# First modulation and projections by quarters of the features, and one round of modulation steps on GpSimd

## What is computed

```python
c_act = silu(c)
for l in range(2):
    mod = c_act @ w_ada[l] + b_ada[l]                # 6 * 1024 columns
    sh1, sc1, gt1, sh2, sc2, gt2 = split(mod, 6)
    h = rmsnorm(x, g_norm1[l]) * (1 + sc1) + sh1
    x = x + gt1 * hybrid_mixer(h, w_in[l], ...)      # four kinds of attention, A to D
    h = rmsnorm(x, g_norm2[l]) * (1 + sc2) + sh2
    x = x + gt2 * grouped_moe(h, ...)
return rmsnorm(x, g_final)
```

## Time and profile before

| | us |
|---|---|
| median of 3 runs | 997.39 (996.74 to 999.74) |
| the profiled execution | 999.34 |
| its span | 997.5 |
| mean granted TensorE clock | 0.983 |
| TensorE busy | 944.5 |
| VectorE busy | 562.0 |
| ScalarE busy | 298.8 |
| GpSimd busy | 61.7 |

### The profile page before, as it was taken

How to read it: one execution, slowest core, us unless ns; L and a number is a source line. 1 busy time by engine, 2 the same in 40 slices (tenths; PEclk the granted TensorE clock), 3 DMA queues, 4 the chain that set the end, 5 groups by cost and what they waited for, 6 DMA issues and landing times.

```text
span 997.5 us, 13699 instructions
## 1 busy us (share of the span) xinstructions
PE 944.5 (95%) x5131; PEld 558.7 (56%) x5131; DVE 562.0 (56%) x1319; ACT 298.8 (30%) x773; POOL 61.7 (6%) x69
## 2 busy tenths in 40 slices
PE   4799999999999899999999999998999979999996
PEld 1344464567644548666754445565774446667572
DVE  1469897779545633223285789785762355223227
ACT  3131224467322221112142122336762122112113
POOL 0001001100000010000300010110000001001012
PEclk9999999999999799999999999999999988999998
DMA  9988417721373789999686471143006058999936
GB/s 352 361 297 280 173 64 253 253 65 46 124 297 95 297 332 404 417 420 367 204 330 239 151 271 64 64 169 24 2 2 274 28 235 310 392 420 420 415 139 235
DMA packets 88529, 231.59 MB, mean 232 GB/s; under 512 B 37768, under 2 KB 52472, under 8 KB 73984
## 3 DMA queue, kind: packets, MB, share of 16 engines
q1 hardware_dynamic: 79536, 198.21, 53.6%
q0 software_dynamic: 5760, 20.97, 5.8%
q10 hardware_dynamic: 3168, 11.54, 2.8%
HBM read 212.85 MB, written 22.57 MB: 236 GB/s over the span
## 4 chain that ended last, share of the span: by engine, by line
PE 87%; DVE 5%; DMA 3%; issue 2%; SPq 1%; POOL 1%; ACT 1%; DVEq 0%; ACTq 0%; POOLq 0%
PE bank L1305 80%; PE bank L1322 5%; PE bank L1642 2%; DMA wbuf<-in_w_ada 2%; DMA shared<-y_rows,ints 1%; DVE shared L826 1%; SPq L1833 1%; DVE x L1258 1%; DVE shared L950 0%; POOL shared L531 0%; DVE x L1267 0%; DVE tok L950 0%; DVE tok L1031 0%; DMA y_rows<-tok 0%; PE bank L1683 0%
## 5 line engine op out<-in xcount | busy, mean ns | idle before, releaser
L1305 PE MATMUL bank<-shared,wbuf 128*128 128x512 f32 (+2 forms) x640 | 239.0, 531 | 0.0
L1305 PE MATMUL bank<-wbuf,shared 128*128 128x512 f32 (+3 forms) x672 | 199.2, 494 | 0.0
L1305 PE MATMUL bank<-shared 128*128 128x128 f32 (+9 forms) x1348 | 183.5, 340 | 1.4 <-ACT tok L567 0.9
L1305 PEld LDWEIGHTS bank<-shared,wbuf 128*128 128x128 f32 (+1 forms) x640 | 109.8, 189 | 123.8 <-issue 115.6
L1305 PEld LDWEIGHTS bank<-shared 128*128 128x128 f32 (+3 forms) x1348 | 138.4, 186 | 46.2 <-issue 40.9
L1305 PEld LDWEIGHTS bank<-wbuf,shared 128*128 128x128 f32 (+1 forms) x672 | 99.5, 178 | 78.6 <-issue 75.0
L1197 DVE TENSOR_TENSOR tring<-bank,tring 128x256 f32<-128x256 f32 x22 | 9.3, 425 | 144.7 <-ACT tring L737 144.7
L567 ACT ACTIVATE shared<-bank 128x512 f32<-128x512 f32 (+3 forms) x60 | 33.7, 561 | 139.7 <-PE bank L1305 138.8
L826 DVE SCALAR_TENSOR_TENSOR shared<-wbuf,small,shared 128x2048 f32<-128x2048 f32 x29 | 69.3, 2388 | 10.4 <-DMA wbuf<-in_w_ada 9.0
L737 ACT ACTIVATE tring<-bank 128x256 f32<-128x256 f32 x22 | 8.5, 384 | 196.7 <-PE bank L1305 196.7
L1305 PE MATMUL bank<-shared,tring 128*128 128x512 f32 x136 | 61.8, 597 | 3.1 <-DVE tring L1243 1.9
(11 more groups left out here) (267 smaller groups left out, 1091.4 us busy)
## 6 DMA issues: line engine op xcount, KB each, us to landing
wbuf<-in_w_ada SPq DMA_DIRECT2D x36, 1024.0 KB, 6.9
shared<-in_w_gate SPq DMA_DIRECT2D x20, 1024.0 KB, 14.8
shared<-in_w_up SPq DMA_DIRECT2D x20, 1024.0 KB, 17.6
shared<-in_w_down SPq DMA_DIRECT2D x20, 1024.0 KB, 16.6
shared<-in_w_ada SPq DMA_DIRECT2D x12, 1024.0 KB, 9.8
wbuf<-in_w_in SPq DMA_DIRECT2D x8, 1536.0 KB, 6.8
wbuf<-in_w_gate SPq DMA_DIRECT2D x12, 1024.0 KB, 7.0
wbuf<-in_w_up SPq DMA_DIRECT2D x12, 1024.0 KB, 10.5
```

What stands on the lines that cost most here:

```text
L1305: return nc.tensor.matmul(dst, lhsT, rhs, start=first, stop=last)
```

## The change

- **The start, layer 0.** x is loaded in two halves. The first 2048 columns of w_ada come by quarters: quarter g is the 256 sh1 columns and the 256 sc1 columns of features 2g and 2g+1 for all 1024 rows, two tiles of 1 MiB, in pieces of 1 KB. Behind each quarter comes a piece of w_in: the rows of features 2g and 2g+1, 672 columns (qD, kvD, qi, ki). The narrow columns come last. hT is first filled with the turned x alone. Quarter 0 goes through TensorE as before; quarters 1 to 3 are eight products each on VectorE (`first_products`), summed over partitions on TensorE (`first_turn`). Then VectorE and ScalarE scale and shift one feature block each in place.
- **The first projections, layer 0.** qi0, qi1, qD0, qD1 and kvD are accumulated in five banks at once, two feature blocks after each quarter (`stream`). kiwi follows, then vDT, cq0, wiT, four scores of block 1, cq1, four scores, ckv. Layer 1 keeps its order.
- **Round 1, both layers.** Steps 8 to 15 leave VectorE. GpSimd does each as a multiply in place and an add (`late_step`), three ahead of the squares of the latents and five behind, before the rotary key. Tiles have five places, two of them in the room of qC, kC and of qA, kA; ScalarE waits for GpSimd's third step before it writes qA. The sum of round 1 on TensorE moves behind vC.
- **SP.** The order of loads follows: in layer 0 chunk 2 of w_in gets room of its own and goes early; tiles 8 and 9 go ahead of tile 3, in layer 1 behind a wait for the end of the combination.
- Some semaphores of VectorE's and ScalarE's own steps are replaced by `link`, which does the same.

The core of the diff:

```diff
+FIRST_COLS = [(OFF["dq"], 672)] + INDEX_PARTS[1:]
+FIRST_BLOCKS = [(("qi", 0), 384), (("qi", 1), 512), (("qD", 0), 0), (("qD", 1), 128), ("kvD", 256)]
+FIRST_KIWI, FIRST_WIDTH = 640, 744
+QUARTERS = 4
...
-ADA_SLOTS = 3
-SLOT_OF = [b % 3 for b in range(14)] + [0, 1] + [b % 2 for b in range(KT)]
+ADA_SLOTS = 5
+SLOT_OF = [b % 3 for b in range(KT)] + [4, 3, 4, 0, 1, 0, 1, 0] + [b % 2 for b in range(KT)]
...
+def steps_to(b):
+
+    return 2 * (b - KT) + 1 if on_pool(b) else b + 1 if b < KT else b - KT + 1
...
+    jobs += [(("qi", m), "act") for m in range(2)]
+    if l == 0:
+        jobs += [(("qD", 0), "act"), (("qD", 1), "act"), ("kvD", "act"), ("kiwi", "act"), ("vDT", "act")]
+        jobs += [(("cq", 0), "act"), ("wiT", "dve")]
+        jobs += idx_jobs(1, ("cq", 1), "ckv")
+    else:
+        jobs += [("kiwi", "act"), (("qD", 0), "act"), ("wiT", "dve")]
+        jobs += idx_jobs(1, ("qD", 1), "kvD")
+        jobs += [(("cq", 0), "act"), ("vDT", "act"), (("cq", 1), "act"), ("ckv", "act")]
...
+        if now[0] == 0 and n == 2:
+            return part(29, 6).rearrange("p h n -> p (h n)").rearrange("p (k n) -> p k n", k=KT)
...
+                def late_step(b):
+
+                    need(pool, ada_landed[SLOT_OF[b]], 16 * (SLOT_OF[0:b].count(SLOT_OF[b]) + 1))
+                    w, k, total = ada_slot(b), b % KT, ada_sum[1]
+                    if k == 0:
+                        nc.gpsimd.tensor_scalar(total, w, cact[:, 0:1], None, ALU.mult).then_inc(late_ada, 1)
+                    else:
+                        nc.gpsimd.tensor_scalar(w, w, cact[:, k:k + 1], None, ALU.mult).then_inc(late_ada, 1)
+                        need(pool, late_ada, 2 * k)
+                        nc.gpsimd.tensor_tensor(total, total, w, ALU.add).then_inc(late_ada, 1)
+
+                if l == 0:
+                    pool.wait_ge(c_ready, 1)
+                for b in range(KT, KT + 3):
+                    late_step(b)
                 for m, name in enumerate([("cq", 0), ("cq", 1), "ckv"]):
                     wait_drained(pool, name)
                     src = cqT[:, m, :] if m < 2 else ckvT
                     nc.gpsimd.tensor_tensor(sqT[:, m, :], src, src, ALU.mult).then_inc(cq_squared, 1)
 
+                for b in range(KT + 3, 2 * KT):
+                    late_step(b)
                 need(pool, cq_squared, 3)
-                need(pool, sum_used, 2)
+                need(pool, sum_used, 1)
                 wait_drained(pool, "kiwi")
                 need(pool, rope_landed, 32)
                 nc.gpsimd.tensor_tensor(krT[0:32, :], krT[0:32, :], cosT[0:32, :], ALU.mult).then_inc(krope_ready, 1)
...
+                    need(act, late_ada, steps_to(KT + 2))
                     drain_pair(("qA", m), qA, m)
...
+
+                for k in range(KT):
+                    wait_first_tile(dve, 2 * g + k // 4)
+                    w = first_tile(2 * g + k // 4)[:, k % 4 * 512:(k % 4 + 1) * 512]
+                    if k == 0:
+                        link(nc.vector.tensor_scalar(first_row, w, cact[:, 0:1], None, ALU.mult))
+                    else:
+                        last = nc.vector.scalar_tensor_tensor(out=first_row, in0=w, scalar=cact[:, k:k + 1], in1=first_row,
+                                                              op0=ALU.mult, op1=ALU.add)
+                        if k < KT - 1:
+                            link(last)
+                last.then_inc(first_row_ready, 1)
...
+                if l == 0:
+                    for k in range(0, KT, 2):
+                        wait_filled(dve, ("h1", k))
+                        nc.vector.tensor_copy(hT[:, k, :], bank(("h1", k))[:, :]).then_inc(dve_drained, 1)
+                    dve.wait_ge(first_turned, 1)
+                    link(nc.vector.tensor_copy(biasT[:, 0:16], banks[7][:, 0:16]))
+                    dve.wait_ge(first_used, 1)
+                    nc.vector.tensor_copy(first_row, banks[6][:, :]).then_inc(first_row_ready, 1)
+                    dve.wait_ge(norm1_landed, 16)
+                    for g in range(QUARTERS):
+                        if g > 0:
+                            first_products(g)
+                        first_scale(g)
+                        k = 2 * g
+                        wait_drained(dve, ("h1", k))
+                        nc.vector.tensor_scalar(hT[:, k, :], hT[:, k, :], scaleT[:, k:k + 1], modT[:, k:k + 1],
+                                                ALU.mult, ALU.add).then_inc(first_h, 1)
...
                 index_sums(1, 0)
                 index_sums(1, 4)
                 dve.wait_ge(consts_landed, CONSTS * 16)
                 top(1)
-                for b in range(KT, 12):
-                    ada_step(b)
                 index_sums(2, 0)
-                for b in range(12, 14):
-                    ada_step(b)
                 index_sums(2, 4)
                 top(2)
                 mod_row(0)
                 index_sums(3, 0)
-                for b in range(14, 2 * KT):
-                    ada_step(b)
...
+
+            def first_turn(g):
+
+                pe.wait_ge(first_row_ready, g + 1)
+                for j in range(4):
+                    at = 64 * (g + 1) + NE * j
+                    last = mm(banks[7][:, at:at + NE], first_row[:, j * P:(j + 1) * P], collect[:, :] if g == 0 else ones[:, 0:NE])
+                last.then_inc(first_rows_turned, 1)
+
+            def stream(k, blocks):
+
+                for name, at in blocks:
+                    last = mm(bank(name)[:, :], first_win[:, k, at:at + P], hT[:, k, :], k == 0, k == KT - 1)
+                    if k == KT - 1:
+                        last.then_inc(psum_filled, 1)
...
+            first_turn(0)
+            for name, _ in FIRST_BLOCKS:
+                wait_bank(pe, name)
+            for g in range(QUARTERS):
+                pe.wait_ge(win_landed[g] if g < 2 else first_win_landed[g - 2], 16)
+                pe.wait_ge(first_h, 2 * g + 2)
+                stream(2 * g, FIRST_BLOCKS)
+                stream(2 * g + 1, FIRST_BLOCKS[0:2])
+                if g < QUARTERS - 1:
+                    first_turn(g + 1)
+                stream(2 * g + 1, FIRST_BLOCKS[2:])
...
+                if l == 0:
+                    need(pe, narrow_landed, (len(INDEX_PARTS) - 1) * 16)
+                    features("kiwi", 104, lambda k: first_win[:, k, FIRST_KIWI:FIRST_KIWI + 104], hT, KT)
+                    turn_vDT()
+                    need(pe, win_landed[2], 16)
+                    project(("cq", 0), 2, 0, P)
+                    turn_wiT()
+                    host(("cq", 1), 2, P, 1, 0)
+                    host("ckv", 2, 256, 1, 4)
...
-                sum_mods(1)
                 wait_drained(pe, ("vA", TT - 1))
...
+                sum_mods(1)
                 need(pe, latents_ready, 1)
...
+            def load_first_ada(n):
+                g, b = divmod(n, 2)
+                columns = w_ada[0:1].rearrange("a (k p) (c n) -> p (a k) c n", p=P, n=D)
+                for c in range(2):
+                    sp.dma_start(first_tile(n).rearrange("p (k c n) -> p k c n", k=4, c=2)[:, :, c, :],
+                                 columns[:, 4 * b:4 * b + 4, c, 2 * g * P:(2 * g + 2) * P]).then_inc(first_ada_landed[max(n - 1, 0)], 16)
+
+            def load_first_win(g):
+                columns = w_in[0:1].rearrange("a (k p) n -> p (a k) n", p=P)
+                first, cols = FIRST_COLS[0]
+                sp.dma_start(first_win[:, 2 * g:2 * g + 2, 0:cols], columns[:, 2 * g:2 * g + 2, first:first + cols])\
+                    .then_inc(win_landed[g] if g < 2 else first_win_landed[g - 2], 16)
...
+            load_x(0)
             sp.dma_start(ident[:, :], k_ident).then_inc(x_landed, 16)
-            sp.dma_start(bada[0:16, :], flat_bias(0, 0, 16)).then_inc(first_bada_landed, 16)
+            load_x(1)
+            sp.dma_start(bada[0:16, :], flat_bias(0, 0, 16)).then_inc(x_landed, 16)
             load_norm1(0)
-            for k in range(KT):
-                load_first_ada(k)
-            load_columns(0, 0)
+            for g in range(QUARTERS):
+                load_first_ada(2 * g)
+                load_first_ada(2 * g + 1)
+                load_first_win(g)
+            load_first_narrow()
...
+                    wait_filled(sp, "kiwi" if l == 0 and n < 5 else chunk_last_job[n - SLOTS])
...
-                        need(sp, ada_used, before_it[-1] + 1)
+                        need(sp, late_ada if on_pool(before_it[-1]) else ada_used, steps_to(before_it[-1]))
...
-                for b in range(3):
-                    load_ada(b)
                 if l == 0:
-                    sp.wait_ge(first_used, KT)
-                load_columns(l, 1)
+                    sp.wait_ge(first_used, 1)
+                    load_ada(0)
+                    load_columns(l, 2)
+                    load_ada(1)
+                    sp.wait_ge(first_row_ready, 2)
+                    load_ada(2)
+                    sp.wait_ge(first_row_ready, 3)
```

(24 more changed lines are left out.)

264 lines of the change are left out of this document (148 added, 116 removed).

## The result

The changed kernel takes **1020.65 us** (median of 6 runs, 1018.03 to 1025.09); the kernel before took 997.28 in the same session. The ratio is 1.0236, 95% interval 1.0205 to 1.0267. I had forecast 991.4. The profiled execution took 1025.09 and is the slowest of the six; its span is 1023.3 where the one of before had 997.5.

The account below looks back on a forecast made before the run. TensorE bounds the kernel (87% of the span), so only its idle time, mainly the start, can be won: 11.55 us less 2.1 for turnings, less a 3.6 stall, is 6.0, giving 991.4 us; range 985.5 to 998.5.

Parts of the forecast that it names:

- What bounds the kernel now: Whole kernel: TensorE bounds 87% of the span, only its idle time can be won, mostly at the start.
- Start of the stream: Layer 0: the first streamed projections on TensorE start at 23.6 us instead of 35.15, 11.55 earlier.
- End: Layer 0: the streamed five blocks, 34.4 us of work plus three turnings of 0.7, end at 60.0.
- Ckv: Layer 0: the ckv projection ends at 90.0 instead of 99.6, 9.6 us won.
- the port: VectorE and GpSimd sharing a port: contention lengthens GpSimd's steps, searches don't contend; no cost in the sum.
- second rival: Sum of round 1, both layers: GpSimd too slow, TensorE stands 19 and 22 us, about 1032; chance 0.10.
- GpSimd's step: Round 1 of the modulation: one multiply and add on GpSimd take 4.2 to 8.4 us, taken as 7; free.
- The search's stall of 3.6: Layer 0 ahead of qA1: the top-128 search holds relu buffers, so TensorE stands 3.6 us, bounds 3.0 and 4.2.
- Chunk aq: Layer 0's w_in load for qA0: issued at 85.2, lands at 91, 0.7 late but hidden; costs only from 94.
- third rival: Layer 0, qA0: chunk aq lands after 94; 3 us late gives 994.5, 6 gives 997.5; chance 0.15.
- Layer 1: Layer 1 keeps its order and stays as long as before; GpSimd's steps there are free.
- The range: Whole time 985.5 to 998.5 us, leaving out the second rival and the lowest of the first rival.

Follow-up runs that it names:

- e11: Changed kernel with GpSimd pieces of 512 columns, chunk aq earlier, small tables issued by ScalarE during the stream, block 2's second four scores behind qA1; 991.8 us, ratio 0.9956.
- e1_thin: Changed kernel with GpSimd's modulation instructions shrunk from 2048 to 16 columns, leaving out most of round 1; 1051.95 us, whole time not comparable.
- e2: Changed kernel's streamed start and layer 0 order, with round 1 of the modulation back on VectorE; 1007.8 us, ratio 1.0117.
- e12: As e11, but with the changed kernel's order of scores: block 2's second four in front of qA1; 1000.4 us, ratio 1.0039.
- e4: Changed kernel with each GpSimd instruction over 2048 columns cut into four pieces of 512; 996.3 us, ratio 0.9991.

## Why the prediction was wrong, step by step

- **What bounds the kernel now: right, but "VectorE is busy there, but nobody waits for it" was carried too far.** It held for before. The change moves the scores to the end of the projections and takes that cover away. Layer 1, which keeps its order, shows the cover: four sums are held there to 8.07 us at 616.7 (2.58 for four in layer 0 before), and TensorE's longest gap in the stage is 0.48.
- **Start of the stream: right, in part by luck.** 23.3 against 23.6. The 16 matmuls on w_ada began 0.6 us earlier than forecast and took 1.9 instead of 2.5; from their end to the stream it was 3.5 us instead of 2.7. **End: 2 us late.** It closes at 62.0 (50.81 + 18.27 less kiwi's 7.13), forecast 60.0: the first 14 matmuls took 7.94, where 20 later ones took 8.83. The granted clock was 0.69 from 23 to 26 and 0.85 from there to 31, a term that the sum didn't have; in the other kernels with this start the same 14 took 7.7 to 9.2. VectorE's products and the 1 KB pieces starved nothing.
- **Ckv: 7.4 us won instead of 9.6, where nothing holds VectorE** (e11: 92.2; the start's 2 us are the difference). In the change itself it is 3.6 lost.
- **The step that failed: the port.** I had the row (1.52 instead of 1.04, and 5.40 instead of 4.70), and put the contention down to GpSimd's pace alone, with "searches, most of VectorE's time there, don't contend". That is true of the searches, to the nanosecond. But the question was which of VectorE's instructions TensorE waits for, and those are the sums and steps between the searches. It cost 23.1 us by wk_v (213.1 against 190.0 in e1_thin) where the forecast had nothing for it and a gain of 6 in all. My second rival had GpSimd held by VectorE and a price at the sum of round 1; what came was the other direction, VectorE held by GpSimd, with its price at the relu buffers. The Trainium skill, SBUF — State Buffer, section Who interferes with whom, says that a VectorE instruction with two SBUF inputs contends with a GpSimd instruction that reads SBUF, and that tensor_scalar can contend in its two-port modes. Of these modes the same section of the Trainium skill says that whoever issues first has the shared ports for the whole instruction and the other "fully blocks". On which instructions are held the trace agrees: L995 has two inputs from SBUF and rose from 618 to 1493 ns, L993 is a tensor-scalar and took 4.37 instead of 0.35, and MAX8 with one input stayed at 428. That a long step beside a multiply ended only 0.41 us after it doesn't fit a full block. I had cited a shorter rule and not this one.
- **GpSimd's step: 10 us instead of 7, and above my upper end of 8.4.** The add was a little over its bound (4.5 to 4.9 against 4.2), the multiply, which I had between 1.3 and 4.2, takes 5.4 at least. That it takes no more than the two-input instruction was a guess and no row bore it. It did no harm: the last step ends at 169.3 where TensorE asks at 201.5, though not "before 150". (The 660 for layer 1 adds 79.6, counted from the start of a square, to 582.3, the end of one; 659 is meant.)
- **The search's stall of 3.6: right mechanism, size as forecast only where the search starts as forecast.** In e2 it is 3.8 once the steps are taken out. In e12 it is 7.2 and 2.4 more for the clock behind it. There the search begins at 91.1, where the scores ahead of ckv (over at 85.6) plus 2.3 gave 87.9; VectorE's last steps end only at 82.9, and its sums are slower beside GpSimd. These 3.2 us come on top of the 3.6. In the change itself it merges with the hold into the 9.1 in front of qA1. I had no term for what a gap does to the clock behind it.
- **Chunk aq: the third rival, hidden in the change, real behind it.** SyncE issued it at 91.06 instead of 85.2; in e4, with VectorE free, at 89.4, and TensorE waited 4.2 us. There the issues took 18.3 us where I had 20.2, but SyncE waited for VectorE's steps until 71, where I had 65: tile 3 was there at 64.8 and not at 60.
- **Layer 1: right.** 155.9 instead of 155.1 us, and e2, which has no GpSimd step, has 155.96 too.
- **The range.** 985.5 to 998.5 left out contention as a large cost: the only rival that had it got 0.10, at another place and price.

What stays open: why pieces of 1024 columns held block 2's sums no longer than pieces of 512 (8.5 and 9.6 us), why a long step beside a multiply is nearly done when the multiply ends and beside an add is not, and where the 3.8 us between the two stages come from. No run here separates these.

## What to carry to other kernels

Before work is moved to GpSimd, list which VectorE instructions the critical engine waits for in the *new* order, and ask of each whether it reads two SBUF tiles or goes from SBUF to SBUF as a tensor-scalar: such an instruction can be held until GpSimd's ends. If it must be moved, cut it: four pieces cost GpSimd 1.3 us per step of 10 and gave back 24 us here. And when an order is changed, an engine's idle cover goes with it; count the free time behind every wait again in the new order before calling anything hidden.
